# Weight slices loaded as halves of 512 KB into a ring of four, in place of slices of 1 MB into a ring of two

## The chip, the cores and the metric

The kernel runs on one core of a Trainium2 chip. The metric is the device time of one execution in microseconds. Three runs of the kernel before took 2225.77 us (median), 2225.76 and 2226.31 us.

## What is computed

The reference is a trunk of two layers on x, 256 positions of width 2048, in float32. Cut to what matters:

```python
for layer in range(DEPTH):                 # DEPTH = 2
    if layer % 2 == 0:
        x = x + even_mixer(rmsnorm(x, e_norm[i]), ...)
    else:
        x = x + conformer_conv(rmsnorm(x, o_norm[i]), ...)
    x = x + sq_relu_mlp(rmsnorm(x, f_norm[layer]), f_w1[layer], f_w2[layer])
return rmsnorm(x, final_norm)

def even_mixer(h, ...):                    # gated DeltaNet beside a spatial-gating MLP
    proj = h @ w_in
    ...
    return jnp.concatenate([out_a, out_b], axis=-1) @ w_out

def conformer_conv(h, pw1, pw1_b, dw, dw_b, ln_g, ln_b, pw2, pw2_b):
    z = h @ pw1 + pw1_b
    z = z[..., :D_MODEL] * jax.nn.sigmoid(z[..., D_MODEL:])
    z = causal_dwconv(z, dw) + dw_b        # width 31
    z = jax.nn.silu(layernorm(z, ln_g, ln_b))
    return z @ pw2 + pw2_b

def sq_relu_mlp(h, w1, w2):                # 2048 to 8192 and back
    a = jax.nn.relu(h @ w1)
    return (a * a) @ w2
```

Nearly all of the work is the products with the weight matrices, 352 chunks of 1 MB and 32 halves of 512 KB, read once each.

## The kernel before

Activations lie transposed, with features on the 128 partitions and the 256 positions along the free axis. A product is done in *groups*: a group makes 512 output features from 2048 input features, over four 1 MB *chunks* of weights (128 partitions x 2048 values, `CH`). A chunk is worked on in two *halves* of 1024 values per partition (`HALF`), so a group has eight halves.

Float32 products are made of reduced-precision parts. Each weight half is split: ScalarE copies it to a rounded high part, `whi` (`high_part`, L341 to L346, the instruction at L346), and VectorE subtracts that from the raw weights to give the low part, `wlo` (`low_part`, from L720, the instruction at L723). TensorE multiplies the high part with both parts of the activation and the low part with the high part of the activation. In `group` (L1246 and L1248) that is 16 matmuls for one half; the cross sums and the main sums lie in different columns of PSUM and ScalarE copies the cross sums out first (`copy_cross`). In `narrow_group` (L1221 to L1225), used for the mixer's projections, it is 24 matmuls.

What sets the order around the change:

- SyncE issues the weight loads, in one program that waits for semaphores in order (from L240). The raw weights have a ring of `RAW` = 2 chunks, `raw[:, r, :]`, with one semaphore `raw_in[r]` for each. `split_chunk(i, r)` (L251 to L254) waits until the low part of the *second* half of the chunk that is in the slot has been made, and then asks for 1 MB.
- `whi` and `wlo` have rings of `SPLIT` = 4 halves each. ScalarE's `high_part` waits for its chunk and then for `half_free`, that is until TensorE has used the half that lay in that place.
- `hi_ready` counts the high parts, which VectorE waits for; `lo_ready` counts the low parts, which TensorE and SyncE wait for.
- ScalarE and VectorE each have one queue in order, written out by hand. `split(G, ...)` puts high and low parts between the other work of a group: the mixer's steps, the copies of the cross sums, squares and reductions of the norms, the residual adds, the gain of the next norm.
- During the first MLP, ScalarE also issues loads and stores of 512 KB (`pre_load`, `pre_store`, L545 to L550), which split half of the pointwise weights ahead of time and write the parts to scratch tensors. SyncE reads them back in the pointwise stage (`pw_load`, L268 and L269). The other half of those weights is taken raw: `pw_chunk` (L271 to L274) loads a chunk once TensorE has finished a group, and `pw1_group` (from L1277) multiplies from `raw` itself (L1316).
- The loop at L294 to L297 serves the second pointwise product and the second MLP; it waits as `split_chunk` does, less the halves of the pointwise stage, which are not split.

Of the kernel before, what the change touches and what calls it, by code (L numbers as in the profile page):

```python
# [25 lines left out]
RAW = 2  # L26
HALF = CH // 2
SPLIT = 4

G_QKVZ, G_UV, G_WOUT, G_MLP0, G_PW1, G_PW2, G_MLP1, G_END = 0, 8, 12, 16, 48, 56, 60, 92  # L30
# [7 lines left out]
UNSPLIT = G_PW2 - G_PW1  # L38
# [32 lines left out]
def build(nc, xt, wts, pw1, w_ba, consts, params, conv_w, dw, rows, w_s, pw_hi, pw_lo, out):  # L71
    with ExitStack() as ctx:
        def sb(name, shape, dt=F32):
            return ctx.enter_context(nc.sbuf_tensor(name, shape, dt))

        def sem(name):
            return ctx.enter_context(nc.semaphore(name))
# [12 lines left out]
        raw = sb("raw", [P, RAW, CH])  # L90
# [54 lines left out]
        pivot = cross[:, 0, :]  # L145


        raw_in = [sem(f"raw_in{i}") for i in range(RAW)]
        table_in, dw_in = sem("table_in"), sem("dw_in")
        const_in, rows_in = sem("const_in"), sem("rows_in")  # L150
        x_again = [sem(f"x_again{j}") for j in range(4)]
# [1 line left out]
        hi_ready, lo_ready = sem("hi_ready"), sem("lo_ready")  # L153
# [84 lines left out]

        @block.sync
        def _(sp):  # L240
            sp.dma_start(pt[:], params).then_inc(const_in, 16)
            sp.sem_inc(pre_low, 1)
            for p in range(2):
                sp.sem_inc(pre_hi_out[p], 16)
                sp.sem_inc(pre_lo_out[p], 16)
            for j in range(4):
                sp.dma_start(x[:, 4 * j:4 * j + 4, :], xt[:, 4 * j:4 * j + 4, :]).then_inc(x_in[j], 16)
                if j < RAW:
                    sp.dma_start(raw[:, j, :], wts[j]).then_inc(raw_in[j], 16)

            def split_chunk(i, r):  # L251

                sp.wait_ge(lo_ready, 2 * (RAW * i + r - RAW + 1))
                sp.dma_start(raw[:, r, :], wts[RAW * i + r]).then_inc(raw_in[r], 16)  # L254

            split_chunk(1, 0)
            for dst, src in ((ct[:], consts), (wba_raw[:], w_ba), (cw[:], conv_w)):
                sp.dma_start(dst, src).then_inc(table_in, 16)
            split_chunk(1, 1)
            sp.dma_start(dwt[:], dw).then_inc(dw_in, 16)  # L260
            with sp.Fori(2, 2 * G_PW1) as i:
                for r in range(RAW):
                    split_chunk(i, r)
            split_chunk(2 * G_PW1, 0)

            def pw_load(half, r):

                sp.dma_start(whi[:, r].rearrange("p a b -> p (a b)").bitcast(F32), pw_hi[half]).then_inc(pw_hi_in[r], 16)  # L268
                sp.dma_start(wlo[:, r].rearrange("p a b -> p (a b)").bitcast(F32), pw_lo[half]).then_inc(pw_lo_in[r], 16)  # L269

            def pw_chunk(g, r):  # L271

                sp.wait_ge(pw_used, 3 * g + 3)
                sp.dma_start(raw[:, r, :], wts[4 * G_PW1 + RAW + g]).then_inc(raw_in[r], 16)  # L274

            for r in range(SPLIT):
                sp.wait_ge(pre_hi_out[r % 2], 16 * (2 + r // 2))
                sp.wait_ge(pre_lo_out[r % 2], 16 * (2 + r // 2))
                sp.wait_ge(half_free, 8 * G_PW1 + r + 1)
                pw_load(r, r)  # L280
                if r == 1:
                    split_chunk(2 * G_PW1, 1)
            for p in range(2):
                sp.wait_ge(pre_hi_out[p], 16 * (PRE // 2 + 1))
                sp.wait_ge(pre_lo_out[p], 16 * (PRE // 2 + 1))
            with sp.Fori(0, KT // 2 - 1) as i:
                for g in range(2):
                    for h in range(2):
                        sp.wait_ge(pw_used, 6 * i + 3 * g + h + 1)
                        pw_load(4 * i + 2 * g + h + SPLIT, 2 * g + h)  # L290
                    pw_chunk(2 * i + g, g)
            for g in range(2):
                pw_chunk(KT - 2 + g, g)
            with sp.Fori(2 * G_PW1 + KT // 2 + 1, 2 * (G_END - UNSPLIT // 2)) as i:  # L294
                for r in range(RAW):
                    sp.wait_ge(lo_ready, 2 * (RAW * i + r - RAW + 1) - 4 * UNSPLIT)
                    sp.dma_start(raw[:, r, :], wts[RAW * i + r]).then_inc(raw_in[r], 16)  # L297
            for n, (a, b) in enumerate(OUT_TILES):
                sp.wait_ge(out_raw, n + 1)
                sp.dma_start(out[:, a:b, :], conv[:, a:b, :]).then_inc(out_done, 16)  # L300
            sp.wait_ge(out_done, 16 * len(OUT_TILES))
# [33 lines left out]
        def _(act):  # L335
# [5 lines left out]
            def high_part(G, i, skipped=0):  # L341

                r = i // 2 % RAW
                act.wait_ge(raw_in[r], 16 * (2 * G - skipped + i // 4 + 1))
                act.wait_ge(half_free, 8 * (G - skipped) + i + 1)
                nc.scalar.activation(whi[:, i % SPLIT].rearrange("p a b -> p (a b)"),  # L346
                                     raw[:, r, HALF * (i % 2):HALF * (i % 2) + HALF], ACT.Copy).then_inc(hi_ready, 1)

            def split(G, *ks, skipped=0):

                for k in ks:
                    if splits_on(G, k):
                        high_part(G, 11 + k, skipped)
                    if side:
                        side_work(16 * G + 16 + 2 * k)
# [41 lines left out]
            for j in range(4):  # L397
                act.wait_ge(xg_raw, j + 1)
                copy(xg[:, 4 * j:4 * j + 4, 0, :], total[:]).then_inc(xg_hi, 1)
                for i in range(2 * j, 2 * j + 2):  # L400
                    high_part(0, i)
            for j in range(4):
                act.wait_ge(x_in[j], 16)
                if j:
                    act.wait_ge(ssum_part, j)
                nc.scalar.activation(padded[:, :, 0:T], x[:, 4 * j:4 * j + 4, :], ACT.Square).then_inc(sq_ready, 1)
                if j < 3:
                    high_part(0, 8 + j)
# [107 lines left out]
            for G in range(G_UV, G_WOUT):  # L516
                i = G - G_UV
# [16 lines left out]
            for j in range(4):  # L534
                G = G_WOUT + j
# [143 lines left out]
            for j in range(4):  # L679
                G = G_PW2 + j  # L680
# [524 lines left out]
        def _(pe):  # L1205
# [71 lines left out]
            def pw1_group(g):  # L1277
# [7 lines left out]
                for i in range(2):  # L1285
                    r = (2 * g + i) % SPLIT
# [11 lines left out]
                            ins = mm(dst, lo[:, cols], woven(xg[:, kt, 0, :]), start=False, stop=False)  # L1298
                    ins.then_inc(pw_used, 1)
                r = g % RAW  # L1300
                pe.wait_ge(raw_in[r], 16 * (2 * G_PW1 + g // 2 + 1))
                for k in range(8):
                    kt = 8 + k
                    if g == 0 and k % 4 == 0:
# [204 lines left out]
            for g in range(KT):  # L1509
                pw1_group(g)  # L1510
# [130 lines left out]
```

## Time and profile before

| | |
|---|---|
| median of three runs | 2225.77 us |
| time of the profiled execution | 2226.43 us |
| span of its instructions | 2224.6 us |
| mean granted clock of TensorE | 0.991 |
| TensorE busy | 2137.2 us, 96% |
| VectorE busy | 1558.0 us, 70% |
| ScalarE busy | 1148.3 us, 52% |
| memory read and written | 427.04 MB and 35.65 MB |

Busy is the time in which an engine has at least one instruction running; matmuls overlap each other and their ends are modelled. A wait is put down to the instruction that came last before it ended. "Before" in a row is the engine's idle time ahead of the instruction. The stages by time: projections and mixer to 521 us, first MLP to about 1205, first pointwise product with the depthwise convolution to 1410, second pointwise product to about 1540, second MLP to the end.

### The profile page before, as it was taken

What the parts mean: (1) busy time and instruction counts of PE and PEld (TensorE: products, weight loads), DVE (VectorE), ACT (ScalarE), POOL (GpSimd) and SP (SyncE); (2) the same over time, 40 slices, a digit from 0 to 9 for tenths busy, and PEclk for the clock granted to TensorE, in tenths of its full rate; (3) what the DMA queues carried; (4) which work ended last, traced back from release to release, by engine and by line L of the source; (5) the groups of instructions that cost most, each with busy time, mean ns of one, the idle gap of its engine ahead of it and who ended that gap; (6) DMA issues with size and microseconds to landing.
All of it is one profiled execution on the core that took longest, in us unless ns stands there. A gap on an engine that the chain in (4) does not pass through costs nothing.

```text
span 2224.6 us, 36337 instructions
## 1 busy us (share of the span) xinstructions
PE 2137.2 (96%) x14192; PEld 1987.6 (89%) x14192; DVE 1558.0 (70%) x1555; ACT 1148.3 (52%) x1457; POOL 37.4 (2%) x56
## 2 busy tenths in 40 slices
PE   7999998999999999999998999898999999999998
PEld 7988898999999989999987999787899999999997
DVE  7767657567766766766776899877766665666666
ACT  4544345444555545545543888754544444444454
POOL 0000000000000000000000012000000000000000
PEclk9999999999999999999999999999999999999999
DMA  6434234355777767777767866245555555555554
GB/s 217 172 128 142 95 114 133 107 209 200 269 273 271 280 254 291 269 270 288 268 254 283 308 243 245 76 154 190 186 207 193 201 205 197 195 205 203 192 207 150
DMA packets 77190, 464.15 MB, mean 209 GB/s; under 512 B 8864, under 2 KB 9248, under 8 KB 32032
## 3 DMA queue, kind: packets, MB, share of 16 engines
q1 hardware_dynamic: 61920, 408.20, 51.2%
q10 hardware_dynamic: 14400, 52.44, 6.0%
q0 software_dynamic: 768, 2.10, 0.5%
q8 instruction: 72, 1.18, 0.2%
q14 instruction: 30, 0.25, 0.0%
HBM read 427.04 MB, written 35.65 MB: 208 GB/s over the span
## 4 chain that ended last, share of the span: by engine, by line
PE 72%; DVE 16%; DMA 5%; ACT 4%; issue 3%; ACTq 0%; SPq 0%; DVEq 0%
PE ps L1246 35%; PE ps L1248 17%; DMA raw<-in_wts 5%; DVE wlo L723 4%; PE ps L1221 3%; PE ps L1225 3%; PE ps L1223 3%; PE ps L1374 3%; PE ps L1316 2%; ACT whi L346 2%; DVE rest L1066 2%; DVE work L1089 1%; DVE rest L1074 1%; DVE sq_part L767 1%; PE ps L1296 1%
## 5 line engine op out<-in xcount | busy, mean ns | idle before, releaser
L723 DVE TENSOR_TENSOR wlo<-raw,whi 128x1024 fp32r<-128x1024 f32 x672 | 815.1, 1223 | 484.0 <-ACT whi L346 470.2
L346 ACT ACTIVATE whi<-raw 128x1024 fp32r<-128x1024 f32 x672 | 700.3, 1056 | 701.7 <-DMA raw<-in_wts 408.6
L1246 PE MATMUL ps<-hid,whi 128*128 128x512 f32 x2240 | 737.7, 383 | 12.4 <-DVE wlo L723 10.0
L1246 PE MATMUL ps<-xg,whi 128*128 128x512 f32 x2048 | 673.5, 383 | 7.4 <-ACT sq_part L391 4.8
L1248 PE MATMUL ps<-hid,wlo 128*128 128x256 f32 x2240 | 611.3, 273 | 0.0
L1248 PE MATMUL ps<-xg,wlo 128*128 128x256 f32 x2048 | 558.9, 273 | 0.0
L1246 PEld LDWEIGHTS ps<-hid,whi 128*128 128x128 f32 x2240 | 424.1, 189 | 75.5 <-DVE wlo L723 10.0
L1246 PEld LDWEIGHTS ps<-xg,whi 128*128 128x128 f32 x2048 | 387.8, 189 | 62.6 <-ACT sq_part L391 5.4
L1248 PEld LDWEIGHTS ps<-hid,wlo 128*128 128x128 f32 x2240 | 430.8, 192 | 0.0
L1248 PEld LDWEIGHTS ps<-xg,wlo 128*128 128x128 f32 x2048 | 393.9, 192 | 0.0
L1221 PE MATMUL ps<-xg,whi 128*128 128x256 f32 x768 | 220.6, 287 | 12.9 <-DVE wlo L723 12.9
L1223 PE MATMUL ps<-xg,whi 128*128 128x256 f32 x768 | 212.7, 277 | 0.0
L1225 PE MATMUL ps<-xg,wlo 128*128 128x256 f32 x768 | 212.5, 277 | 0.0
L1221 PEld LDWEIGHTS ps<-xg,whi 128*128 128x128 f32 x768 | 148.9, 194 | 13.0 <-issue 11.8
L1223 PEld LDWEIGHTS ps<-xg,whi 128*128 128x128 f32 x768 | 148.9, 194 | 0.0
L1225 PEld LDWEIGHTS ps<-xg,wlo 128*128 128x128 f32 x768 | 148.9, 194 | 0.0
L632 ACT ACTIVATE prods<-work,dwt 128x256 f32<-128x256 f32 x368 | 148.5, 494 | 0.0
L741 DVE TENSOR_TENSOR total<-ps,cross 128x1024 f32<-128x1024 f32 x67 | 98.8, 1475 | 55.9 <-ACT cross L339 52.8
L1316 PE MATMUL ps<-work,raw 128*128 128x256 f32 x512 | 113.5, 379 | 0.0
L1316 PEld LDWEIGHTS ps<-work,raw 128*128 128x128 f32 x512 | 96.1, 190 | 12.4
L339 ACT ACTIVATE cross<-ps 128x1024 f32<-128x1024 f32 (+1 forms) x66 | 65.5, 992 | 65.0 <-PE ps L1248 64.5
L1296 PE MATMUL ps<-xg,whi 128*128 128x256 f32 x256 | 74.0, 289 | 2.7 <-DMA wlo<-pw_lo 2.7
(237 smaller groups left out, 2046.4 us busy)
## 6 DMA issues: line engine op xcount, KB each, us to landing
raw<-in_wts SPq DMA_DIRECT2D x352, 1024.0 KB, 4.8
pre_raw<-in_pw ACTq DMA_DIRECT2D x32, 512.0 KB, 7.5
pw_hi<-pre_hi ACTq DMA_DIRECT2D x32, 512.0 KB, 5.9
pw_lo<-pre_lo ACTq DMA_DIRECT2D x32, 512.0 KB, 6.8
whi<-pw_hi SPq DMA_DIRECT2D x32, 512.0 KB, 4.2
wlo<-pw_lo SPq DMA_DIRECT2D x32, 512.0 KB, 5.5
x<-in_xt SPq DMA_DIRECT2D x4, 512.0 KB, 8.6
x<-in_xt ACTq DMA_DIRECT2D x4, 512.0 KB, 3.6
```

The lines of the kernel that those rows point to most:

```text
L346: nc.scalar.activation(whi[:, i % SPLIT].rearrange("p a b -> p (a b)"), raw[:, r, HALF * (i % 2):HALF * (i % 2) + HALF], ACT.Copy).then_in ...
L632: ins = nc.scalar.activation(dst, window(g, k), ACT.Copy, scale=w)
L723: tt(wlo[:, i % SPLIT].rearrange("p a b -> p (a b)"), raw[:, i // 2 % RAW, HALF * (i % 2):HALF * (i % 2) + HALF], whi[:, i % SPLIT].rearra ...
L741: tt(halves(total[:]), in_order(ps[:, 4 * par:4 * par + 4, 0:T]), in_order(cross[:]), ALU.add).then_inc(banks_free, 1)
L1221: mm(dst, whi[:, r, k, cols], woven(operand[:, kt, 0, :]), start=(kt == 0 and n % 2 == 0), stop=False, skip_group_check=True)
L1223: mm(dst, whi[:, r, k, cols], woven(operand[:, kt, 1, :]), start=False, stop=False, skip_group_check=True)
L1225: ins = mm(dst, wlo[:, r, k, cols], woven(operand[:, kt, 0, :]), start=False, stop=(kt == KT - 1), skip_group_check=True)
L1246: mm(ps[:, 4 * par + n, :], whi[:, r, k, cols], woven_parts(operand[:, kt]), start=(kt == 0), stop=False)
L1248: ins = mm(ps[:, 4 * par + n, T:2 * T], wlo[:, r, k, cols], woven(operand[:, kt, 0, :]), start=False, stop=(kt == KT - 1))
L1296: mm(dst, hi[:, cols], woven(xg[:, kt, 0, :]), start=(kt == 0), stop=False)
L1316: ins = mm(ps[:, par + n, 0:T], raw[:, r, cols], xf[:, kt, :], start=False, stop=(kt == KT - 1))
L1374: ins = mm(bank(b)[:, h, :], left[:, h, :], right[:, h, :], start=True, stop=True)
```

## The change

The ring of raw weights keeps its size, 2 x 1 MB, but is taken as four halves with a semaphore each. SyncE issues two transfers of 512 KB for each chunk. In `split_chunk` each of them waits for the low part of the half that lies in its own place. In `pw_chunk` both are issued after the one wait. ScalarE's `high_part` waits for its own half alone; TensorE, which reads a whole raw chunk in `pw1_group`, waits for both. The rings of `whi` and `wlo`, and the order of work on ScalarE, VectorE and TensorE, stay as they are. A row of a transfer becomes 4 KB for each partition, out of a row of 8 KB in memory.

```diff
@@ -145,7 +145,7 @@
         pivot = cross[:, 0, :]
 
 
-        raw_in = [sem(f"raw_in{i}") for i in range(RAW)]
+        raw_in = [sem(f"raw_in{i}") for i in range(SPLIT)]
         table_in, dw_in = sem("table_in"), sem("dw_in")
         const_in, rows_in = sem("const_in"), sem("rows_in")
         x_again = [sem(f"x_again{j}") for j in range(4)]
@@ -238,6 +238,11 @@
 
         @block.sync
         def _(sp):
+            def load_half(chunk, r, h):
+
+                part = slice(HALF * h, HALF * h + HALF)
+                sp.dma_start(raw[:, r, part], wts[chunk][:, part]).then_inc(raw_in[2 * r + h], 16)
+
             sp.dma_start(pt[:], params).then_inc(const_in, 16)
             sp.sem_inc(pre_low, 1)
             for p in range(2):
@@ -246,12 +251,14 @@
             for j in range(4):
                 sp.dma_start(x[:, 4 * j:4 * j + 4, :], xt[:, 4 * j:4 * j + 4, :]).then_inc(x_in[j], 16)
                 if j < RAW:
-                    sp.dma_start(raw[:, j, :], wts[j]).then_inc(raw_in[j], 16)
-
-            def split_chunk(i, r):
-
-                sp.wait_ge(lo_ready, 2 * (RAW * i + r - RAW + 1))
-                sp.dma_start(raw[:, r, :], wts[RAW * i + r]).then_inc(raw_in[r], 16)
+                    for h in range(2):
+                        load_half(j, j, h)
+
+            def split_chunk(i, r, apart=0):
+
+                for h in range(2):
+                    sp.wait_ge(lo_ready, 2 * (RAW * i + r) + h - 2 * RAW + 1 - apart)
+                    load_half(RAW * i + r, r, h)
 
             split_chunk(1, 0)
             for dst, src in ((ct[:], consts), (wba_raw[:], w_ba), (cw[:], conv_w)):
@@ -271,7 +278,8 @@
             def pw_chunk(g, r):
 
                 sp.wait_ge(pw_used, 3 * g + 3)
-                sp.dma_start(raw[:, r, :], wts[4 * G_PW1 + RAW + g]).then_inc(raw_in[r], 16)
+                for h in range(2):
+                    load_half(4 * G_PW1 + RAW + g, r, h)
 
             for r in range(SPLIT):
                 sp.wait_ge(pre_hi_out[r % 2], 16 * (2 + r // 2))
@@ -293,8 +301,7 @@
                 pw_chunk(KT - 2 + g, g)
             with sp.Fori(2 * G_PW1 + KT // 2 + 1, 2 * (G_END - UNSPLIT // 2)) as i:
                 for r in range(RAW):
-                    sp.wait_ge(lo_ready, 2 * (RAW * i + r - RAW + 1) - 4 * UNSPLIT)
-                    sp.dma_start(raw[:, r, :], wts[RAW * i + r]).then_inc(raw_in[r], 16)
+                    split_chunk(i, r, 4 * UNSPLIT)
             for n, (a, b) in enumerate(OUT_TILES):
                 sp.wait_ge(out_raw, n + 1)
                 sp.dma_start(out[:, a:b, :], conv[:, a:b, :]).then_inc(out_done, 16)
@@ -341,7 +348,7 @@
             def high_part(G, i, skipped=0):
 
                 r = i // 2 % RAW
-                act.wait_ge(raw_in[r], 16 * (2 * G - skipped + i // 4 + 1))
+                act.wait_ge(raw_in[i % SPLIT], 16 * (2 * G - skipped + i // 4 + 1))
                 act.wait_ge(half_free, 8 * (G - skipped) + i + 1)
                 nc.scalar.activation(whi[:, i % SPLIT].rearrange("p a b -> p (a b)"),
                                      raw[:, r, HALF * (i % 2):HALF * (i % 2) + HALF], ACT.Copy).then_inc(hi_ready, 1)
@@ -1298,7 +1305,8 @@
                             ins = mm(dst, lo[:, cols], woven(xg[:, kt, 0, :]), start=False, stop=False)
                     ins.then_inc(pw_used, 1)
                 r = g % RAW
-                pe.wait_ge(raw_in[r], 16 * (2 * G_PW1 + g // 2 + 1))
+                for h in range(2):
+                    pe.wait_ge(raw_in[2 * r + h], 16 * (2 * G_PW1 + g // 2 + 1))
                 for k in range(8):
                     kt = 8 + k
                     if g == 0 and k % 4 == 0:
```

## Rows read from the trace of the kernel before

**Rows 1.** The page, part 1: busy us (share of the span) xinstructions.

```profile
PE 2137.2 (96%) x14192; PEld 1987.6 (89%) x14192; DVE 1558.0 (70%) x1555; ACT 1148.3 (52%) x1457; POOL 37.4 (2%) x56
```

**Rows 2.** Who waited for whom, whole span: us in total, times, longest us.

```profile
ACT whi L346 <- DMA raw<-in_wts: 408.6, 177, 6.2
...
PE ps L1246 <- DVE wlo L723: 11.0, 12, 2.2
...
PE ps L1246 <- ACT sq_part L391: 4.8, 2, 4.0
```

**Rows 3.** Stretches: us; busy PE, PEld, DVE, ACT, POOL (xcount); clock; DMA share; GB/s.

```profile
1750.00:2000.00 250.00, 250.00 (x1529) 229.86 (x1528) 163.62 (x134) 119.27 (x114) 0.00 (x0) 1.00 0.56 201
1140.00:1192.00 52.00, 45.86 (x262) 40.51 (x261) 36.59 (x30) 25.43 (x27) 0.00 (x0) 0.97 0.57 212
1495.00:1566.00 71.00, 61.96 (x361) 55.14 (x360) 51.20 (x43) 34.56 (x41) 0.00 (x0) 0.98 0.48 176
795.00:835.00 40.00, 38.62 (x234) 35.02 (x234) 25.03 (x21) 18.11 (x19) 0.00 (x0) 1.00 0.73 270
1205.00:1215.00 10.00, 7.30 (x50) 7.31 (x51) 7.19 (x6) 3.07 (x3) 0.00 (x0) 0.83 1.02 419
850.00:1000.00 150.00, 150.00 (x918) 138.02 (x917) 105.22 (x88) 75.62 (x76) 0.00 (x0) 1.00 0.76 276
```

**Rows 4.** The chain of waits, 795 to 1190: start us, us, what.

```profile
797.32 6.89 DMA raw<-in_wts
...
1152.17 6.67 DMA raw<-in_wts
...
1176.79 8.14 DMA raw<-in_wts
```

**Rows 5.** Timeline, 1495 to 1562: start, us, engine, line, what [idle before <-releaser].

```profile
1502.26 1.23 DVE L723 TENSOR_TENSOR wlo<-raw,whi 128x1024 fp32r<-128x1024 f32 x1
...
1503.55 0.48 PE L1246 MATMUL ps<-hid,whi 128*128 128x512 f32 x1 [0.79 <-DVE wlo L723]
...
1504.66 3.65 DVE L723 TENSOR_TENSOR wlo<-raw,whi 128x1024 fp32r<-128x1024 f32 x3
...
1510.84 1.07 ACT L346 ACTIVATE whi<-raw 128x1024 fp32r<-128x1024 f32 x1 [3.96 <-DMA raw<-in_wts]
...
1511.81 1.55 ACT L373 ACTIVATE cross<-ps,pt 128x256 f32<-128x256 f32 x4
...
1548.74 1.23 DVE L723 TENSOR_TENSOR wlo<-raw,whi 128x1024 fp32r<-128x1024 f32 x1
...
1557.79 1.06 ACT L346 ACTIVATE whi<-raw 128x1024 fp32r<-128x1024 f32 x1 [4.56 <-DMA raw<-in_wts]
```

**Rows 6.** Timeline, 437 to 449, VectorE and TensorE.

```profile
439.03 1.22 DVE L723 TENSOR_TENSOR wlo<-raw,whi 128x1024 fp32r<-128x1024 f32 x1 [2.63 <-ACT whi L346]
...
448.74 1.01 PE L1471 MATMUL ps<-work 128*128 128x128 f32 x3 [3.38 <-DVE work L973]
```

**Rows 7.** The page, part 6: DMA issues, xcount, KB each, median us to landing.

```profile
raw<-in_wts SPq DMA_DIRECT2D x352, 1024.0 KB, 4.8
pre_raw<-in_pw ACTq DMA_DIRECT2D x32, 512.0 KB, 7.5
...
whi<-pw_hi SPq DMA_DIRECT2D x32, 512.0 KB, 4.2
```

**Rows 8.** The page, part 3: queue, packets, MB, share of 16 engines.

```profile
q1 hardware_dynamic: 61920, 408.20, 51.2%
q10 hardware_dynamic: 14400, 52.44, 6.0%
q0 software_dynamic: 768, 2.10, 0.5%
```

**Rows 9.** The tile raw: SyncE's issues, ns min/median/max; and SyncE's longest wait.

```profile
L254 SPq DMA_DIRECT2D raw<-in_wts x192: 328/333/480, 12.9 to 1200.7; - x192
...
SPq L254 <- DVE wlo L723: 1052.9, 191, 13.6
```

## The prediction

> **What bounds the kernel now.** I read the busy times first. TensorE is busy 96% of the span [rows 1], so whatever is saved has to come out of its idle time: 2224.6 less 2137.2, or 87 us. Next, who waited for whom over the whole span [rows 2]. ScalarE, which makes the high part of each weight half, waited 408.6 us for weight transfers, but TensorE waited only 11.0 us in 12 places for a low part and 4.8 us for the root of a norm, once 4.0 and once 0.8. So most of ScalarE's wait is hidden: a chunk that comes late uses up slack and TensorE never sees it. The question is where it does see it.
>
> For that I took stretches [rows 3]. Where nothing is late (1750 to 2000) TensorE issues 1529 matmuls in 250 us, 0.1635 us each, so a half (16 matmuls) takes 2.62 us and four halves 10.46 us. A stretch's width less its count times 0.1635 is what TensorE loses there, idle time and a lowered clock together. It gives: 1140 to 1192, 52 - 262 x 0.1635 = 9.2 us; 1495 to 1566, 71 - 361 x 0.1635 = 12.0 us; 795 to 835, 40 - 234 x 0.1635 = 1.7 us. The first two are the last quarter of the first MLP and the second pointwise product with the start of the second MLP. In both, each group is followed by residual and norm work on VectorE. The clock matters: it was 0.97 and 0.98 over these two stretches, 1.00 where TensorE never paused.
>
> Then the chain of waits inside 1140 to 1192 [rows 4]. The transfer issued at 1152.17 takes 6.67 us to land, and the next on the chain 8.14 us from 1176.79, although it is the same 1 MB. The timeline of 1495 to 1562 [rows 5] shows why TensorE feels it. ScalarE's queue is in order, and the copy of the cross sums out of PSUM stands behind a high part. TensorE starts the seventh half of a group at 1503.55, right after its low part of 1502.26, and ends the eighth two halves later, at 1508.8. The high part ahead of the copy starts at 1510.84, after 3.96 us of waiting for its chunk, so the copy starts at 1511.81, 3.0 us late. VectorE's residual and norm work hang on that copy, and the low parts that TensorE needs next lie between them.
>
> **The change, part by part.** (a) *When a half is asked for.* Before, both halves of a slot are requested after the low part of the second. After, each follows its own. In [rows 5] the low part of the first half ends at 1502.26 + 1.23 = 1503.49, that of the second at 1504.66 + 1.23 = 1505.89: the first is asked for 2.4 us earlier. The second is asked for when it was.
>
> (b) *How long a half takes.* 1 MB lands 4.8 us after issue (median); the 512 KB from the scratch tensors 4.2 us [rows 7]. At the 419 GB/s that the core moves when its queues are full (1205 to 1215, [rows 3]), half a megabyte is 1.25 us less data, so 3.5 us. Bounds: 3.5 and, under contention, the 7.5 us of the 512 KB loads that ScalarE issues [rows 7]. I take 3.5 to 4.2. The half that ScalarE waits for in front of the copy is always the first of its chunk, so it comes 2.4 + 0.6 to 1.3 = 3.0 to 3.7 us earlier than now, against 3.0 us by which the copy is late.
>
> (c) *1495 to 1566, 12.0 us.* With the copy at the end of the group, VectorE's work moves up by 3.0 us. The waits that TensorE has for low parts there are about 1 us each, so these go. At the end of the stretch the high part of 1557.79 waited 4.56 us, and the root, behind it in ScalarE's queue, kept TensorE for its longest wait there (4.0 us, [rows 2]) and brought the clock down. That half would be asked for after the low part of 1548.74, at 1550, and land by 1554. What is late next is the root itself, and the other wait for a root was 0.8 us. Saved 12.0 - 0.9 = 11.1 us; bounds 5.5 (half) and 12.0.
>
> (d) *1140 to 1192, 9.2 us.* The same structure, with ScalarE's copies for the pointwise weights (1.5 MB per group) on the other queue, which is what stretches 4.8 us to 6.67 and 8.14 [rows 4]. An earlier request of half the size has mostly landed when those begin. Saved 8.5 us; bounds 0 (the copies delay the halves as much) and 9.2.
>
> (e) *795 to 835, 1.7 us.* The chain runs through a chunk there too, 6.89 us from 797.32 [rows 4]. Saved 1.7; bounds 0 and 1.7.
>
> (f) *Mixer, at 440 to 456* [rows 6]. The high part came late, so VectorE stood 2.63 us ahead of its low part at 439.03, with the group norm's reductions behind it; TensorE then waited 3.38 us for them. The half is again the first of its chunk. VectorE can win its 2.63 us, less what the high part must wait for TensorE to free its buffer. I take 2.3, bounds 0 and 3.4.
>
> (g) *The start of the pointwise stage, 1205 to 1215.* The queues are full (share 1.02), the clock is 0.83. The first weight half of that stage is late. Raw halves asked for earlier leave 1.25 us less data ahead of it. I take 1.0; bounds 0 and 4.2 (the 2.7 us that TensorE is idle, 10 - 7.30, and 1.5 us of clock).
>
> (h) *Added.* 352 transfers more, 0.333 us each to issue, 117 us on SyncE's queue, which stood 1052.9 us for low parts in its first loop alone [rows 9]; hidden by that. Its waits come in the order in which the low parts are made, so none blocks a later request. In the pointwise stage TensorE reads the raw chunk itself and now waits for both halves; both are still asked for together after the group, some 20 us ahead of their use, so nothing. At the start the x pieces are issued behind one transfer more each, at most 0.8 us; the first piece is not, and the later ones wait behind VectorE: nothing, bounds 0 and 0.8 us lost. Rows of 4 KB instead of 8 KB: 52.44 MB in 4 KB rows cost 6.0% of the engines, 408.20 MB mostly in 8 KB rows 51.2% [rows 8], 8.7 and 8.0 MB per point, so no dearer. If the cover in (h) were gone, it would cost 0.333 us per half on the path.
>
> Sum: 11.1 + 8.5 + 1.7 + 2.3 + 1.0 = 24.6 us. The profiled execution took 2226.43 us, so 2201.8; the median of the runs is 0.66 lower, 2201.2.
>
> Against the smaller size the rows show that half the bytes save only 0.6 us of 4.8 [rows 7], most of a transfer's time being no data. A rule of the Trainium skill says so too (DMA: Bandwidth & Descriptors, section Bandwidth): batch transfers to at least 1 MiB. Its fit in the section Anatomy of one DMA, 2.0 us and the bytes at 436 GB/s, makes an estimated 4.4 us of a megabyte and 3.2 of a half. If the 2.0 us overlap, the sum by the page is the same 24.6; if they hold the queues, four halves take an estimated 12.8 us, longer than TensorE needs for them, and the change loses some hundred us. What the trace makes of that is the slower rival.
>
> **The rivals.** *VectorE's own chain is late next* (0.20). With the copy on time, the norm work may still hold low parts back: reduction, sum, two multiplications and four low parts fill much of a group, and VectorE is the busiest after TensorE there (51.20 of 71 us, [rows 3]). For it: the waits named in [rows 5] run through VectorE. Against: 3 us of room for waits of 1 us. Then half of (c) and (d) stays: gain 5.5 + 4.6 + 1.7 + 2.3 + 0.5 = 14.6, 2211.2 us.
>
> *The copies of the pointwise weights hold the halves up as well* (0.10). Then (d), (e) and (g) stay: gain 11.1 + 2.3 = 13.4, 2212.4 us. For it: 6.67 and 8.14 us. Against: the first half would be asked for before such a burst begins and has half as many bytes to bring in.
>
> *Hidden anyway* (0.04). The halves come early and TensorE's waits are all VectorE's: 2225.8 us. This would also be the time if the request of the first half stood behind something else on SyncE. Against: 4.56 and 3.96 us of ScalarE's wait stand next to TensorE's.
>
> *Slower: small transfers fill the queues* (0.04). GpSimd's queue moved 2.10 MB for 0.5% [rows 8], 4.2 MB per point, twice q1's price. If 4 KB rows on SyncE's queue cost that, the weights' share (0.56 at 201 GB/s, [rows 3]) doubles. From 850 to 1000 the share is 0.76 at full TensorE pace; it would be 1.32, and TensorE would run at the pace of the queues: 0.32 x 620 us of the first MLP and 0.12 x 630 us of the second, 270 us, 2496 us. It decides from 0.24 of free share over 0.56, that is from 1.43 times today's price per byte; just above that, the loss is a few us. Against: q10 moves its rows at the lower price, and 419 GB/s were reached mostly with 4 KB rows.
>
> The page of the Trainium skill named above calls most of its fixed part completion latency, which would not hold the queues; by that the trace agrees, at 419 GB/s.
>
> **How the numbers follow.** The forecast has 0.62. Its own bounds are 2225.8 - 3.4 - 1.7 - 9.2 - 4.2 - 12.0 = 2195.3 and, upward, the two rivals at 2211 and 2212. The range is 2195 to 2213. A measurement of this kernel can tell 0.2%, some 4.5 us, from no change. Faster by more: 0.62 + 0.20 + 0.10 = 0.92; the same: 0.04; slower: 0.04.
>
> **What the profile after would show.** Transfers of 512 KB with a median under 4.3 us; ScalarE's wait for weights well under 408.6 us; TensorE's waits for a low part under 3 us in all; the wait for the root under 1 us; over 290 matmuls in each 48 us of the norm stages, at clock 1.00. I am wrong if the copies of cross sums still start 3 us after their group, if a half takes as long as a chunk did, or if the share of the queues from 850 to 1000 rises.

## The result and the profile after

The changed kernel takes 2192.23 us (median of four runs, 2190.48 to 2195.24), the kernel before 2225.77 us beside it. The ratio is 0.9851, 95% interval 0.9836 to 0.9867: 33.5 us faster. The prediction had 2201.2 us and a range of 2195 to 2213. The direction and most of the mechanism hold; the gain is 8.9 us larger than forecast, and the time lies 2.8 us below the range.

The busy times, part 1 of the page of the changed kernel:

```profile
PE 2126.3 (97%) x14192; PEld 1981.6 (90%) x14192; DVE 1561.1 (71%) x1555; ACT 1155.2 (53%) x1457; POOL 38.2 (2%) x56
```

The span is 2192.0 us, so TensorE's idle time fell from 87 to 66 us [rows 1], and its busy time by 11 us although it does the same 14192 matmuls. That fits fewer matmuls at a lowered clock: the mean granted clock is 0.994, after 0.991.

Who waited for whom, over the whole span:

```profile
ACT whi L353 <- PE ps L1255: 480.0, 366, 2.2
...
ACT cross L346 <- PE ps L1255: 101.3, 60, 7.3
...
ACT whi L353 <- DMA raw<-in_wts: 21.1, 12, 4.5
```

ScalarE's wait for weights fell from 408.6 to 21.1 us [rows 2]. In its place stands TensorE: a high part now waits until TensorE frees its buffer. TensorE has no row left with a wait for a low part in the MLPs (11.0 us before); its 11.7 us at the very start remain. The chain that ended last, part 4 of the page, by engine, has no weight transfer in it any more (5% before):

```profile
PE 83%; DVE 12%; ACT 3%; issue 1%; DMA 0%; DVEq 0%; SPq 0%; ACTq 0%
```

The stretches that answer to [rows 3], chosen by the place in the work (columns: us; busy us of PE, PEld, DVE, ACT, POOL with counts; granted clock; DMA share; GB/s):

```profile
1740.00:1990.00 250.00, 250.00 (x1528) 229.90 (x1528) 160.75 (x132) 118.11 (x114) 0.00 (x0) 1.00 0.61 200
1127.70:1171.00 43.30, 43.30 (x266) 39.81 (x265) 35.26 (x30) 24.41 (x25) 0.00 (x0) 1.00 0.75 266
1473.00:1534.00 61.00, 60.63 (x369) 55.16 (x368) 49.19 (x41) 35.25 (x40) 0.00 (x0) 1.00 0.60 199
785.00:825.00 40.00, 40.00 (x247) 36.77 (x246) 25.78 (x22) 19.69 (x19) 0.00 (x0) 1.00 0.79 274
1182.00:1195.00 13.00, 10.62 (x69) 10.07 (x68) 7.22 (x6) 3.07 (x3) 0.00 (x0) 0.87 1.02 406
850.00:1000.00 150.00, 150.00 (x918) 138.02 (x917) 106.37 (x88) 78.15 (x76) 0.00 (x0) 1.00 0.78 275
```

By the same count as in the prediction, at 0.1635 us for a matmul, TensorE now loses nothing from 1127.7 to 1171 (266 matmuls are 43.5 us) and from 785 to 825, and 61 - 369 x 0.1635 = 0.7 us from 1473 to 1534. The clock is 1.00 in all three.

Transfers and queues, parts 6 and 3 of the page:

```profile
raw<-in_wts SPq DMA_DIRECT2D x704, 512.0 KB, 4.7
pre_raw<-in_pw ACTq DMA_DIRECT2D x32, 512.0 KB, 10.4
...
whi<-pw_hi SPq DMA_DIRECT2D x32, 512.0 KB, 5.3
```

```profile
q1 hardware_dynamic: 112608, 408.22, 55.6%
q10 hardware_dynamic: 14400, 52.44, 6.0%
```

A half lands 4.7 us after its issue (median), hardly less than the 4.8 us of the 1 MB [rows 7]. The median hides the stages. In the projections and the mixer (0 to 521 us) a half took 3.9 us and the 1 MB before 4.8; in the first MLP (543 to 1190), beside the transfers that ScalarE issues, both took 5.3; in the second MLP (1540 to 2200) 4.5 and 4.8. SyncE's queue moves the same bytes for 55.6% of the engines over 2192.0 us instead of 51.2% over 2224.6 us [rows 8]. That is 7% more of the engines' time for each byte.

The copy of the cross sums that answers to the one in [rows 5], on ScalarE's timeline:

```profile
1484.47 1.06 ACT L353 ACTIVATE whi<-raw 128x1024 fp32r<-128x1024 f32 x1 [1.94 <-DMA raw<-in_wts]
1486.65 1.57 ACT L380 ACTIVATE cross<-ps,pt 128x256 f32<-128x256 f32 x4 [1.11 <-PE ps L1255]
```

The high part ahead of the copy waits 1.94 us for its half, and it no longer matters: the copy itself then waits 1.11 us for TensorE's group to end.

**Where the time went.** The clearest view is to set the start of the same matmul in the two timelines side by side, here the first of a half, and see by how much the changed kernel leads. The letters are the terms of the prediction:

| place | before, us | after, us | lead, us | gained since | forecast |
|---|---|---|---|---|---|
| fourteenth group, first half | 456.92 | 448.46 | 8.5 | 8.5 | 2.3 (f) |
| second group of the first MLP | 543.64 | 534.17 | 9.5 | 1.0 | 0 |
| thirty-first group, fifth half | 828.51 | 817.13 | 11.4 | 1.9 | 1.7 (e) |
| forty-eighth group, fourth half | 1191.57 | 1170.83 | 20.7 | 9.4 | 8.5 (d) |
| start of the second pointwise product | 1443.70 | 1422.40 | 21.3 | 0.6 | 1.0 (g) |
| second MLP, second half of its second group | 1564.96 | 1532.30 | 32.7 | 11.4 | 11.1 (c) |
| end of the span | 2224.6 | 2192.0 | 32.6 | 0.0 | 0 |

Four terms are right to within 1 us in this pair of traces. The first line is wrong by 6.2 us, and the second was not expected at all. In a second trace of the changed kernel the first line is 7.0 us and (g) is 3.0 us; the others differ by at most 0.2 us.

### The profile page after: what moved, and what is told of

It reads as the page before. It is cut to its first block, busy times and chain, and to the rows that moved or that the text cites. A ratio compares the mean times of both kernels' runs of the same rounds, so it can differ in the third digit from the quotient of the medians.

```text
span 2192.0 us, 37722 instructions
## 1 busy us (share of the span) xinstructions
PE 2126.3 (97%) x14192; PEld 1981.6 (90%) x14192; DVE 1561.1 (71%) x1555; ACT 1155.2 (53%) x1457; POOL 38.2 (2%) x56
## 3 DMA queue, kind: packets, MB, share of 16 engines
q1 hardware_dynamic: 112608, 408.22, 55.6%
## 4 chain that ended last, share of the span: by engine, by line
PE 83%; DVE 12%; ACT 3%; issue 1%; DMA 0%; DVEq 0%; SPq 0%; ACTq 0%
PE ps L1253 43%; PE ps L1255 21%; PE ps L1228 3%; PE ps L1232 3%; PE ps L1230 3%; PE ps L1382 3%; DVE wlo L730 3%; PE ps L1324 2%; DVE rest L1073 2%; ACT whi L353 1%; DVE work L1096 1%; DVE rest L1081 1%; PE ps L1303 1%; PE ps L1305 1%; PE ps L1304 1%
## 5 line engine op out<-in xcount | busy, mean ns | idle before, releaser
L1228 PE MATMUL ps<-xg,whi 128*128 128x256 f32 x768 | 220.7, 287 | 11.7 <-DVE wlo L730 11.7
L1228 PEld LDWEIGHTS ps<-xg,whi 128*128 128x128 f32 x768 | 148.9, 194 | 11.8 <-issue 11.7
## 6 DMA issues: line engine op xcount, KB each, us to landing
pre_raw<-in_pw ACTq DMA_DIRECT2D x32, 512.0 KB, 10.4
```

What stands on the lines that cost most here:

```text
L1228: mm(dst, whi[:, r, k, cols], woven(operand[:, kt, 0, :]), start=(kt == 0 and n % 2 == 0), stop=False, skip_group_check=True)
```

## The experiments

Each run is given with the median of the kernel before beside it and the ratio with its 95% interval.

**Half of the mixer's error: one place alone.** The step of 8.5 us is not at 440 to 456 alone; 3.5 us of it is at 123 us, where TensorE waits for a scaling on VectorE (L900). On ScalarE's and TensorE's timelines before:

```profile
113.77 2.00 ACT L346 ACTIVATE whi<-raw 128x1024 fp32r<-128x1024 f32 x2 [4.46 <-PE ps L1225]
```

```profile
123.13 1.77 PE L1399 MATMUL ps<-x_space,ct 128*128 128x512 f32 x2 [4.01 <-DVE x_space L900]
```

ScalarE's 4.46 us are put down to TensorE. But the view names what came last, and two things came at one moment: the chunk landed at 113.75, and a half on TensorE ended at 113.76, which is not the one the high part needed (that ended at 111.1). I had gone by the name. To settle it, halves for the first 18 chunks only (pairs 0 to 8), and 1 MB chunks after that:

```diff
+STAGE, HALVES_FIRST = 9, True
...
+            def load_chunk(chunk, r):
+
+                sp.dma_start(raw[:, r, :], wts[chunk]).then_inc(chunk_in[r], 16)
...
+                if (i < STAGE if isinstance(i, int) else pairs_early[0]) == HALVES_FIRST:
                     for h in range(2):
+                        sp.wait_ge(lo_ready, 2 * (RAW * i + r) + h - 2 * RAW + 1 - apart)
+                        load_half(RAW * i + r, r, h)
+                else:
+                    sp.wait_ge(lo_ready, 2 * (RAW * i + r - RAW + 1) - apart)
+                    load_chunk(RAW * i + r, r)
```

> Halves for the first 18 chunks only (up to about 135 us), then 1 MB chunks as before. At 113.77 before, the wait of ScalarE of 4.46 us is put down to TensorE, whose half had ended at 113.76, but the chunk had landed at 113.75 and the half whose place was needed had been used at 111.1. Theory A (the wait was for the chunk): the high part moves up by 2.5 us, TensorE's wait near 121 us falls from 4.0 to about 1.8 us, its clock from 114 to 130 is 1.00 instead of 0.89, and the total is 3 to 4 us less: 2221.5 to 2223 us. Theory D (the wait was TensorE's own, as the view has it): no change there, 2225 to 2226 us.

Measured: 2221.83 us (before 2225.53), ratio 0.9983 [0.9973, 0.9994]. The stretch 114 to 130, before, changed kernel and this run (the second row of each of the first two is the mixer's other place):

```profile
114.00:130.00 16.00, 11.99 (x87) 10.76 (x87) 12.96 (x17) 9.34 (x13) 0.00 (x0) 0.89 0.45 168
440.00:456.00 16.00, 12.19 (x84) 11.74 (x84) 11.52 (x17) 5.79 (x7) 0.00 (x0) 0.79 0.50 176
```

```profile
114.00:130.00 16.00, 14.06 (x119) 13.15 (x118) 14.67 (x20) 11.74 (x15) 0.00 (x0) 1.00 0.44 146
434.00:450.00 16.00, 12.81 (x112) 12.46 (x112) 11.27 (x15) 7.23 (x9) 0.00 (x0) 1.00 0.66 220
```

```profile
114.00:130.00 16.00, 14.06 (x118) 13.15 (x118) 14.44 (x19) 10.42 (x14) 0.00 (x0) 1.00 0.44 162
```

In the same 16 us TensorE does 87 matmuls before and 118 with halves for 18 chunks, and the clock is 1.00 instead of 0.89. In the changed kernel the high part starts at 111.32 and TensorE's wait is 1.81 us:

```profile
111.32 1.06 ACT L353 ACTIVATE whi<-raw 128x1024 fp32r<-128x1024 f32 x1 [2.93 <-PE ps L1232]
```

```profile
121.08 1.12 PE L1407 MATMUL ps<-x_space,ct 128*128 128x512 f32 x2 [1.81 <-DVE x_space L907]
```

The wait was for the chunk. The same step, 3.3 to 3.5 us, turns up in the trace of each run that has halves in the mixer, except the one in which every half is asked for later (below). At the other place (440 to 456) TensorE's wait fell from 3.38 to 1.54 us and the clock went from 0.79 to 1.00. The 1.8 us of the wait are less than the 2.3 forecast; the clock is the rest of the 3.1 us, and the prediction left it out.

That this run as a whole is 3.7 us faster is partly luck. Its trace is 3.5 us up at 123 us, only 0.2 us ahead at the first MLP (1.6 us went with the clock from 380 to 400, which was 1.00 in the trace before and 0.91 here), and gains 3.8 us in the last quarter of the first MLP, where it loads 1 MB as before.

**All of the mixer, and all of the rest.** Halves for the first 64 chunks and 1 MB after that; and the complement. The edit is the same with another boundary.

> Halves, each asked for on its own, for the projections, the mixer and its output product (the first 64 chunks); 1 MB chunks with the waits of before from the first MLP on. Comparing the two traces half by half, the changed kernel is 8.5 us ahead when the first MLP begins. Theory A (that lead is made in the mixer by chunks that no longer come late, and stays to the end): 2215.5 to 2219 us. Theory of the prediction, term (f): only the place at 440 to 456 gives, 2.3 us: 2222 to 2225 us.

Measured: 2213.95 us (before 2225.53), ratio 0.9945 [0.9925, 0.9965]: 11.6 us, more than the 8.5 of the mixer and 1.5 us below the time of theory A, though the interval (8 to 17 us) holds the 8.5. The trace is 6.9 us ahead at the first MLP and gains 4.4 us later, where it loads as before. A start shifted against the other queue's transfers may meet them at other moments; no run shows that this is the reason. The theory of 2.3 us falls.

> The complement of the run with halves in the mixer: 1 MB chunks with the waits of before for the first 64 chunks, halves from the first MLP on. If the gains of the stages add (each stage's late chunks are its own), this has the whole less the 8.5 us that the traces give to the projections and the mixer: 2199 to 2203 us, and half by half the trace is level with before up to 520 us. If a lead made early only reappears as a wait later (stages do not add), this alone gives 2190 to 2196 us.

Measured: 2203.98 us (before 2224.05), ratio 0.9916 [0.9899, 0.9932]: 20.1 us, some 4 less than the 24.2 of the table, just above the expected range. Half by half the trace is level with before up to 520 us (within 1.3 us) and then takes the steps of the changed kernel, 1.0 us at the root after the first norm among them. The medians of the stages add to within the intervals: 11.6 + 20.1 = 31.7 us against 33.5.

**What of the change does it: the size or the moment?** First the size alone, both halves of a slot asked for when its second has been split:

```diff
-                for h in range(2):
-                    sp.wait_ge(lo_ready, 2 * (RAW * i + r) + h - 2 * RAW + 1 - apart)
-                    load_half(RAW * i + r, r, h)
+                sp.wait_ge(lo_ready, 2 * (RAW * i + r) - 2 * RAW + 2 - apart)
+                for h in range(2):
+                    load_half(RAW * i + r, r, h)
```

> Two transfers of 512 KB for each chunk, as in the changed kernel, but both are asked for when the second half of the slot has been split, as before the change. Theory A (the first half of a chunk is what holds ScalarE up, and it comes early mostly because it is asked for 2.4 us earlier): the first half then lands about 1.1 us sooner than the 1 MB did (3.7 against 4.8 us), so about a third of the 33.5 us is gained: 2210 to 2218 us, and ScalarE's wait for weights lies between 21 and 408 us, nearer to the upper. Theory B (the smaller transfer is what helps, whenever it is asked for): 2190 to 2200 us, wait under 60 us.

Measured: 2207.42 us (before 2225.53), ratio 0.9921 [0.9902, 0.994]: 18.1 us, over half of the whole and more than theory A allowed, far less than theory B. ScalarE's wait, and its timeline at the place of [rows 5]:

```profile
ACT whi L353 <- DMA raw<-in_wts: 219.5, 127, 4.6
```

```profile
1470.55 1.06 ACT L353 ACTIVATE whi<-raw 128x1024 fp32r<-128x1024 f32 x1 [3.21 <-DMA raw<-in_wts]
1471.51 1.55 ACT L380 ACTIVATE cross<-ps,pt 128x256 f32<-128x256 f32 x4
```

The wait is halved. At this place 3.21 us are left, 0.75 less than before, and the copy follows at once: it is still the chunk that holds it. So the first half landing about 1 us sooner is worth 18 us, and its being asked for earlier another 15.

Then the requests of the changed kernel, but ScalarE waits for both halves of the chunk:

```diff
-                act.wait_ge(raw_in[i % SPLIT], 16 * (2 * G - skipped + i // 4 + 1))
+                for h in range(2):
+                    act.wait_ge(raw_in[2 * r + h], 16 * (2 * G - skipped + i // 4 + 1))
```

> The changed kernel, but ScalarE starts on either half of a chunk only when both halves have landed. Requests and transfers are as in the changed kernel. Theory A (the first half being there alone is the gain): the second half is asked for when the 1 MB was and lands about as late, so nearly nothing is left: 2219 to 2226 us, ScalarE's wait above 300 us. Theory C (spreading the bytes over time takes pressure off the queues and everything lands sooner): 2190 to 2205 us.

Measured: 2215.18 us (before 2225.53), ratio 0.9951 [0.9932, 0.9969]: 10.4 us. Its waits:

```profile
ACT whi L354 <- DMA raw<-in_wts: 341.1, 148, 4.8
...
PE ps L1254 <- DVE wlo L731: 9.9, 10, 2.5
```

Most of the gain is gone, and TensorE waits 9.9 us for low parts again (11.0 before). That the first half may be used alone is worth 23 of the 33.5 us. The 10 that stay are more than theory A gave; the second half, 512 KB with its first half mostly in already, lands a little sooner than a 1 MB did (median 4.65 us against 4.8). Theory C falls.

Last the opposite, every half asked for one low part later than its own:

```diff
-                    sp.wait_ge(lo_ready, 2 * (RAW * i + r) + h - 2 * RAW + 1 - apart)
+                    due = 2 * (RAW * i + r) + h - 2 * RAW + 2 - apart
+                    sp.wait_ge(lo_ready, min(due, 8 * G_PW1) if isinstance(i, int) else due)
```

> The changed kernel with every half asked for one low part later than its own: the first half of a slot when the 1 MB was asked for before the change (as in the run where both are late), the second one low part later still, some 2.6 us. Theory A' (what matters is when the first half of a chunk comes; the second has 2.6 us more until it is wanted): as with both late, 2205 to 2211 us. Theory F (both halves are equally near to their use, and what counts is the lead of each): clearly slower than that run, 2212 to 2224 us, with ScalarE's wait for weights above 300 us.

Measured: 2248.28 us (before 2225.77), ratio 1.0098 [1.0073, 1.0124], slower than the kernel before by 22.5 us. Theory A' falls; F had the direction and the wait, but not that it would be slower than before. Its waits:

```profile
ACT whi L354 <- DMA raw<-in_wts: 511.5, 334, 4.7
...
PE ps L1254 <- DVE wlo L731: 25.5, 38, 2.0
```

Now both halves are late: ScalarE waits 334 times, TensorE 38 times for a low part. My sentence "the second has 2.6 us more until it is wanted" was wrong, because that second half is what the *next* request waits for.

**Place by place.** The same comparison of matmul starts with the trace before, for each of these runs (us gained, minus is lost; times are those of the trace before):

| run | 113 to 136 | 439 to 457 | first root, 457 to 544 | (e) 544 to 829 | (d) 829 to 1192 | (c) 1444 to 1565 |
|---|---|---|---|---|---|---|
| changed kernel, both traces | 3.5 | 3.1 | 1.0 | 1.9 | 9.4 | 11.4, 11.2 |
| halves in 18 chunks | 3.5 | 0.4 | -0.3 | 0.7 | 3.8 | -0.9 |
| halves in the first 64 chunks | 3.5 | 3.1 | 0.2 | 1.8 | 3.3 | -1.1 |
| halves after them | -0.5 | -0.1 | 1.0 | 1.9 | 9.2 | 11.3 |
| both halves asked for late | 3.3 | 1.9 | 1.0 | 1.9 | 6.6 | 3.8 |
| ScalarE waits for both | 3.5 | 2.1 | 0.8 | 1.8 | -2.9 | 2.0 |
| every half one later | -0.1 | 1.8 | -0.2 | -9.7 | -13.2 | -0.3 |

In the mixer, at the first root and in (c) the gain is there where halves are loaded and nearly gone where they are not. In (c) most of it needs the early request: 3.8 us without it, 11.4 with it. In (e) and (d) it is less clear. Two runs that load 1 MB there gain 0.7 and 1.8 us in (e), 3.8 and 3.3 in (d) over the one trace before. Part of these two terms is thus how that one execution went, and not the change.

**A loop fits the order.** The load of a place is a loop: low part made, request, landing, high part (1.06 us), low part (1.22 us), and it has to close in four halves of TensorE, 10.46 us. Before, the first half's loop is 2.6 (one low part) + 4.8 + 2.3 = 9.7 us, 0.8 us of slack, and a landing that stays above 5.6 us breaks it. With the change it is 4.7 + 2.3 = 7.0, slack 3.5. With both late it is 2.6 + 3.8 (issued at 1466.70, used at 1470.55 above) + 2.3 = 8.7, slack 1.8. With everything one later both halves have 2.6 + 4.7 + 2.3 = 9.6, where before the second had a slack over 3 us. Slack and time go together: 3.5, 1.8 and 0.8 us against 2192, 2207 and 2226. This sum is argued from the rows, not shown by itself; that the runs fall in this order is shown. A late half delays its own next request, so a microsecond counts more than once; with everything one later, 22.9 us were lost in the first MLP, where a half took 4.9 us to land.

The sum ranks the runs and does not find the places. Before, 11 of the 30 chunks asked for from 850 to 1000 took over 5.6 us, and TensorE lost nothing there, so a single late chunk does not cost it time. From 1495 to 1566, where it lost 12.0 us, one of 12 took over 5.6. There VectorE's norm work stands between the low parts; the sum leaves that out, and how much it matters was not measured.

**The price of 4 KB rows.** The weights laid out so that each half is one block in memory:

```diff
-                sp.dma_start(raw[:, r, part], wts[chunk][:, part]).then_inc(raw_in[2 * r + h], 16)
+                sp.dma_start(raw[:, r, part], wts[chunk, h]).then_inc(raw_in[2 * r + h], 16)
...
-        "wts": np.concatenate(parts, 0),
+        "wts": np.concatenate(parts, 0).reshape(-1, P, 2, HALF).transpose(0, 2, 1, 3),
```

> The changed kernel with the weights laid out in memory so that each half is one contiguous block of 512 KB (before: 4 KB out of every 8 KB row of a chunk). SyncE's queue moved 8.0 MB per point of share with 8 KB rows and 7.3 with the 4 KB rows of the changed kernel. Theory A (the price is that of 4 KB packets, wherever they lie): share and time as in the changed kernel, 55 to 56% and 2190 to 2196 us. Theory E (the price is the stride in memory): the share falls back to about 51%; the time is still the same, as nothing waits for the queues' rate.

Measured: 2191.52 us (before 2224.05), ratio 0.986 [0.9843, 0.9877]. From its page:

```profile
q1 hardware_dynamic: 112608, 408.22, 54.5%
...
raw<-in_wts SPq DMA_DIRECT2D x704, 512.0 KB, 4.0
```

The landing falls from 4.7 to 4.0 us, so the stride costs landing time. The share falls by 1.1 points of the 4.4 that the change had added, but the last run below has the same layout, lands in 4.0 us again and has a share of 55.5%. That the stride costs any share is therefore not shown; most of the added share stays with 4 KB rows wherever they lie, near theory A. The total does not move by what can be measured: with 3.5 us of slack, 0.7 us more is not needed.

**A version beyond both.** The start is now the largest single wait (11.7 us): a table load of 1.28 us on ScalarE stands behind the first piece of x.

```diff
             act.wait_ge(const_in, 16)
+            copy(flat_small[:, 0:1], eps)
             for j in range(4):
                 act.wait_ge(xg_raw, j + 1)
```

> The changed kernel with one small copy more at the head of ScalarE's queue, so that the table load of 1.28 us that stood behind the first x piece (at 6.8 us) is done while that piece is under way. TensorE's first matmul then starts at 10.5 instead of 11.7 us, and the total is 1.2 us less than the changed kernel beside it if the start is on the path; no less if the start is hidden by the later norm sum near 43 us (VectorE's chain begins only with the piece's landing, so that it too should move up).

Measured: 2192.89 us, ratio 0.9866 [0.985, 0.9883]. ScalarE's timeline:

```profile
0.75 1.28 ACT L346 ACT_TABLE_LOAD   x1 [0.75 <-PEq L1643]
...
6.49 1.06 ACT L346 ACTIVATE xg<-total 128x1024 fp32r<-128x1024 f32 x1 [3.50 <-DVE total L813]
```

The table load is done at 2.0 us, the first copy starts at 6.49 instead of 8.07, and TensorE starts at 10.17 instead of 11.74. The changed kernel itself, beside the same runs of before:

> The changed kernel unaltered, on the same chip as the run with the early table load, to have both beside the same runs of before: 2190 to 2195 us. Where executions of it differ from the first trace, the clock in the stretches 40 to 52 and 375 to 395 should differ (1.00 or 0.86 and 0.91), and nothing else by over 1 us.

Measured: 2193.54 us, ratio 0.9872 [0.9855, 0.9888]. The median is 0.65 us lower with the early load, less than either interval resolves. In its trace TensorE still leads by 1.5 us at 113 us, so the start is not hidden there. What differs between executions is the clock, as expected: the stretch 375 to 395 in the first trace of the changed kernel and in this one.

```profile
375.00:395.00 20.00, 15.59 (x135) 15.02 (x134) 8.21 (x10) 7.09 (x9) 0.00 (x0) 1.00 0.25 80
```

```profile
375.00:395.00 20.00, 15.59 (x121) 15.02 (x120) 7.55 (x9) 6.43 (x8) 0.00 (x0) 0.91 0.19 61
```

The same work and idle time, 135 matmuls in one and 121 in the other. But the transition to the pointwise product also differed, by over 2 us between the traces (the lead at 1443.70 was 21.3 us in the first and 22.3 in this one, which was 1.5 us behind it at the end of the mixer), so "nothing else by over 1 us" was wrong.

Both together:

> The changed kernel with each half contiguous in memory and with the early table load together. The early table load put TensorE's first matmul 1.6 us earlier in its trace; the contiguous halves landed in 4.0 instead of 4.7 us and ScalarE's wait for weights fell to 9 us. Expected 1.5 to 3 us below the changed kernel beside the same runs of before: ratio 0.985 to 0.986, 2188 to 2192 us. If the lead at the start is lost at the norm sum near 43 us: 2191 to 2194 us.

Measured: 2190.51 us (before 2225.77), ratio 0.9842 [0.9822, 0.9862], inside the 2188 to 2192 us expected; the span of its trace is 2189.0. ScalarE's wait for weights:

```profile
ACT whi L353 <- DMA raw<-in_wts: 9.7, 5, 4.4
```

This is the lowest median of all, 35.3 us below before, but its interval holds the changed kernel's ratio of 0.9851; that it is faster than that one is not shown.

## Why the prediction was wrong in size and right in kind

- *What bounds the kernel, and that most of ScalarE's wait is hidden:* right. Of 387.5 us of wait that went, 33.5 reached the time.
- *(a) and (b):* the request 2.4 us earlier is right and was worth 15 us, by the run with both late. The landing of 3.5 to 4.2 us was right in the mixer (3.9) and wrong over the whole: 4.7, and 5.3 in the first MLP. 609 of the 704 halves were asked for while an earlier one was under way, 142 of the 352 chunks before; that this is the reason is not shown. The upper bound held for the median. The half in front of the copy took 3.7 us (1480.74 to 1484.45), with no earlier half under way.
- *(c), (d), (e):* 11.4, 9.4 and 1.9 us against 11.1, 8.5 and 1.7. The count of matmuls in a stretch, less what the full rate gives, was a good measure of what could be gained. For (c) the runs bear the term out. That (d) and (e) came out so close is partly luck, as runs with 1 MB loads there had up to 3.8 and 1.8 us of them too. In (c), what was "late next" was smaller than I had put it, 0.4 us for the root.
- *(f), the step that failed:* 8.5 us instead of 2.3. The mixer was sized at one place. I left out the place at 123 us (3.5 us with its clock), because the trace put ScalarE's wait down to TensorE, and two small ones at 280 and 355 us (about 1 us each, absent in the runs that load 1 MB there; what waits there was not looked into). At the place I had, 3.1 us came, as the clock came back with the wait. In the second trace the mixer gave 7.0 us, the same steps less 1.6 us of clock from 375 to 395. The bound of 3.4 us was a bound on that place, not on the stage. I had counted lost matmuls for the MLPs and not for the mixer; 114 to 130 would have shown 87 where 119 fit.
- *Not in the sum:* 1.0 us at the second group of the first MLP. I took the 0.8 us wait for the first root as what is left when no chunk is late. ScalarE's timeline before shows a chunk in front of that one too, and the changed kernel no wait for weights there. The run with 1 MB from there on gains 0.2 us at this place, the one with halves from there on 1.0:

```profile
542.17 1.06 ACT L346 ACTIVATE whi<-raw 128x1024 fp32r<-128x1024 f32 x1 [3.89 <-DMA raw<-in_wts]
...
543.13 0.46 ACT L391 ACTIVATE sq_part<-ps,pt 128x256 f32<-128x256 f32 x1
```

```profile
531.81 1.06 ACT L353 ACTIVATE whi<-raw 128x1024 fp32r<-128x1024 f32 x1 [2.00 <-PE ps L1255]
...
532.77 0.46 ACT L398 ACTIVATE sq_part<-ps,pt 128x256 f32<-128x256 f32 x1
```

- *(g):* 0.6 us against 1.0 in this trace, 0.9 in the run with halves after the mixer, 3.0 to 4.1 in four later traces that also have halves there. Inside the bounds of 0 and 4.2, and not the same from one execution to the next.
- *(h):* the 352 transfers more cost nothing on SyncE's queue, as said. That 4 KB rows are no dearer was wrong: 7% more of the engines' time for each byte.
- *The rivals:* VectorE's chain as the next bound did not come about. The other queue's copies did slow the halves, to 5.3 us in the first MLP, and got slower themselves (pre_raw from 7.5 to 10.4 us), but TensorE lost nothing in (d) and (e) by it. The slower case needed 1.43 times the price per byte; it was 1.07, and the share from 850 to 1000 went from 0.76 to 0.78. (The time of the first rival took half of 9.2 us for (d) where half of 8.5 was meant: 2211.5 us, not 2211.2.) The rule of at least 1 MiB (the Trainium skill, DMA: Bandwidth & Descriptors, section Bandwidth) is about bandwidth. The queues' price agrees with it, at 7% more per byte. This kernel's time hangs on when a half is there, and the share stays under 0.8 where TensorE runs at full pace. The fit in the section Anatomy of one DMA, from which the prediction estimated 3.2 us for a half, is stated by the Trainium skill for transfers that GpSimd issues; SyncE's landed in 3.9 to 5.3 us by stage.
- *The signs named beforehand:* ScalarE's wait (21.1 us), the low parts in the MLPs (none), the root (0.4 us) and the matmuls of the norm stages (266 in 43.3 us, 369 in 61 us) came as said. The half's median under 4.3 us did not. Two of the three signs of being wrong turned up: over the whole run a half took as long as a chunk had, and the share from 850 to 1000 rose. Both are about the transfers' cost, and neither decided the time.
- *The range:* its lower end was made of bounds of single places, and the mixer's stood too narrow, so the range missed by 2.8 us.

## What to carry to other kernels

Where loads, conversion and use form a ring, write the loop of one place down with its durations and compare it with the time in which it must close; look for the losses where other work stands in that loop, and count when a part is *asked for* as well as its size (15 and 18 us here). Count matmuls per stretch against the full rate in every stage before sizing a term, and read a wait that is put down to TensorE with the landing times beside it, as two events within 10 ns can carry the wrong name. Compare more than one pair of traces place by place, against a run that leaves the place alone, before a term is called right. A wait on TensorE costs more than its idle time where the clock falls after it.

## What was not expected of the hardware

- Halving a transfer did not halve its landing: over the whole run 4.8 us for 1 MB, 4.7 for 512 KB in 4 KB rows out of 8 KB, 4.0 for 512 KB in one block. In the mixer it was 4.8 against 3.9 us, in the first MLP 5.3 for both sizes.
- The clock after a pause of TensorE is not the same in each execution. After the waits of up to 2.4 us from 375 to 395 it was 1.00 in one trace and 0.91 in another of the same kernel, which is 14 matmuls in 20 us, and the second trace lost 1.6 us of its lead there. This can be part of the spread of 2 to 5 us between runs.
- Pauses of 4.01 and 3.38 us in the mixer came with a clock of 0.89 and 0.79 over 16 us; with the pauses at 1.81 and 1.54 us it was 1.00 in both. The first of these places cost 3.5 us where 2.2 us of idle time went.
